# The level masks of a blockwise triangular inverse, applied by VectorE on the way out of PSUM

## The reference

```python
kk = jnp.einsum("bhncd,bhnsd->bhncs", k, k)
lower = jnp.where(strict, beta[..., :, None] * kk * decay, 0.0)
a_mat = jnp.broadcast_to(eye, lower.shape) + lower
sol = lax.linalg.triangular_solve(a_mat, rhs, left_side=True, lower=True, unit_diagonal=True)
```

## Time and profile before

| | |
|---|---|
| median of 3 runs | 3048.26 us (3047.57 to 3049.72) |
| profiled execution | 3046.6 us, span 3044.8 us |
| mean granted TensorE clock | 0.981 |
| TensorE busy | 2850.4 us, 94% of the span |
| GpSimd busy | 1728.8 us, 57% |
| VectorE busy | 1324.1 us, 43% |
| ScalarE busy | 1172.8 us, 39% |

### The profile page before, as it was taken

How to read it: one execution, slowest core, us unless ns; L and a number is a source line. 1 busy time by engine, 2 the same in 40 slices (tenths; PEclk the granted TensorE clock), 3 DMA queues, 4 the chain that set the end, 5 groups by cost and what they waited for, 6 DMA issues and landing times.

```text
span 3044.8 us, 37926 instructions
## 1 busy us (share of the span) xinstructions
PE 2850.4 (94%) x14376; PEld 2380.5 (78%) x14376; DVE 1324.1 (43%) x1864; ACT 1172.8 (39%) x2040; POOL 1728.8 (57%) x1324
## 2 busy tenths in 40 slices
PE   1799979999999999999999999999999999889998
PEld 1588767888888788888888788887888888668886
DVE  4555655353535335553434525545343432421123
ACT  2133443353444434353343433444333333343332
POOL 2254555575656656576555665657565655566554
PEclk9889999999999999999999999999999999999999
DMA  5521322222232323422233222422222222423332
GB/s 221 228 80 56 101 67 68 82 80 81 81 116 90 101 70 103 140 73 93 74 104 104 90 87 87 143 78 86 79 87 80 80 82 92 142 76 97 97 97 84
DMA packets 86581, 295.10 MB, mean 97 GB/s; under 512 B 10240, under 2 KB 10240, under 8 KB 82304
## 3 DMA queue, kind: packets, MB, share of 16 engines
q1 hardware_dynamic: 64944, 247.05, 25.6%
q10 hardware_dynamic: 21456, 45.62, 4.5%
HBM read 276.90 MB, written 15.73 MB: 96 GB/s over the span
## 4 chain that ended last, share of the span: by engine, by line
PE 83%; DVE 6%; POOL 5%; issue 2%; DMA 2%; ACT 2%; SPq 0%; ACTq 0%; POOLq 0%; DVEq 0%
PE acc L392 23%; PE acc L394 22%; PE acc L393 22%; PE pm L426 7%; PE pm L431 3%; DMA mixing<-in_ada_w 2%; POOL w L1388 1%; DVE mixing L1018 1%; POOL mT L1397 1%; ACT io L636 1%; PE pm L408 1%; PE pm L545 1%; DVE x L1257 1%; PE pm L518 1%; DVE io L934 1%
## 5 line engine op out<-in xcount | busy, mean ns | idle before, releaser
L1388 POOL TENSOR_TENSOR w<-raw,w 128x512 fp32r<-128x512 f32 x832 | 1116.4, 1344 | 1047.3 <-ACT w L610 1019.1
L610 ACT ACTIVATE w<-raw 128x512 fp32r<-128x512 f32 x832 | 521.0, 627 | 783.2 <-PE acc L394 662.3
L392 PE MATMUL acc<-mT,w 128*128 128x512 f32 x1280 | 517.3, 404 | 13.0 <-POOL mT L1397 5.8
L394 PE MATMUL acc<-mT,w 128*128 128x512 f32 x1280 | 501.6, 392 | 0.0
L393 PE MATMUL acc<-mT,w 128*128 128x512 f32 x1280 | 500.4, 391 | 0.0
L392 PE MATMUL acc<-hT,w 128*128 128x512 f32 x1024 | 437.1, 427 | 41.4 <-POOL w L1388 30.8
L394 PE MATMUL acc<-hT,w 128*128 128x512 f32 x1024 | 407.8, 398 | 0.0
L393 PE MATMUL acc<-hT,w 128*128 128x512 f32 x1024 | 406.7, 397 | 0.0
L1229 DVE SCALAR_TENSOR_TENSOR x<-acc,ab,x 128x512 f32<-128x512 f32 x256 | 191.4, 750 | 450.3 <-PE acc L394 450.1
L392 PE MATMUL acc<-hid,w 128*128 128x512 f32 x896 | 364.4, 407 | 13.8 <-POOL hid L1402 8.3
L394 PE MATMUL acc<-hid,w 128*128 128x512 f32 x896 | 350.3, 391 | 0.0
(11 more groups left out here) (201 smaller groups left out, 3828.0 us busy)
## 6 DMA issues: line engine op xcount, KB each, us to landing
raw<-in_w_all SPq DMA_DIRECT2D x416, 512.0 KB, 3.6
mixing<-in_ada_w SPq DMA_DIRECT2D x24, 1024.0 KB, 7.3
xr<-in_xT ACTq DMA_DIRECT2D x48, 256.0 KB, 2.9
out<-io ACTq DMA_DIRECT2D x32, 256.0 KB, 2.6
mixed_kept<-mixing ACTq DMA_DIRECT2D x28, 256.0 KB, 2.0
xr<-mixed_kept ACTq DMA_DIRECT2D x28, 256.0 KB, 2.7
x<-in_xT ACTq DMA_DIRECT2D x6, 1024.0 KB, 7.3
x<-in_xT SPq DMA_DIRECT2D x1, 2048.0 KB, 17.4
```

The costliest lines, as they stand in the source:

```text
L392: e.matmul(bank, whi, x[:, 0, :], start=first, stop=False)
L394: m = e.matmul(bank, wlo, x[:, 0, :], start=False, stop=last)
L610: e.activation(w2[:, 0, local % HALVES, :], raw[:, tile % NRAW, local % 2 * NT:(local % 2 + 1) * NT], ACT.Copy).then_inc(S["w_hi"], 1)
L1388: e.tensor_tensor(w2[:, 1, local % HALVES, :], raw[:, tile % NRAW, local % 2 * NT:(local % 2 + 1) * NT], w2[:, 0, local % HALVES, :].bitca ...
```

## The change

GpSimd no longer masks the operand. TensorE multiplies the whole `LT` by `T`, ScalarE's copy of that product goes away, and VectorE takes it out of PSUM with the mask of the level, `X = bE * lmask[l]`. The masks of levels 1 to 6 are those of the lower left blocks now, no longer transposed. The wait in front of the query convolution is on `x_out` in place of `lvl_mask`. The copy of `U` stays on ScalarE.

```diff
 TensorE, mix
                 if 22 <= s <= 42 and s % 4 == 2:
                     l = (s - 22) // 4 + 1
-                    e.wait_ge(S["lvl_mask"], (LEVELS - 1) * n + l)
                     if l == 1:
                         e.wait_ge(S["t_ready"], n + 1)
+                        e.wait_ge(S["lt_ready"], n + 1)
...
-                    four(bE, Lm, T).then_inc(S["x_out"], 1)
+                    four(bE, LT, T).then_inc(S["x_out"], 1)
 ScalarE, mix
-                if 22 <= s <= 42 and s % 4 == 2:
+                if 26 <= s <= 42 and s % 4 == 2:
                     l = (s - 22) // 4 + 1
-                    if l > 1:
-                        e.wait_ge(S["y_out"], (LEVELS - 1) * n + l - 1)
-                        e.wait_ge(S["t_turned"], (LEVELS - 2) * n + l - 1)
-                        e.activation(U, bF, ACT.Copy).then_inc(S["u_turned"], 1)
-                    e.wait_ge(S["x_out"], (LEVELS - 1) * n + l)
-                    e.activation(X, bE, ACT.Copy).then_inc(S["x_ready"], 1)
+                    e.wait_ge(S["y_out"], (LEVELS - 1) * n + l - 1)
+                    e.wait_ge(S["t_turned"], (LEVELS - 2) * n + l - 1)
+                    e.activation(U, bF, ACT.Copy).then_inc(S["u_turned"], 1)
 VectorE, front
                 if s == 42:
-                    e.wait_ge(S["lvl_mask"], (LEVELS - 1) * m)
+                    e.wait_ge(S["x_out"], (LEVELS - 1) * m)
                     conv(m, 1, GQ, (0, 1))
 VectorE, mix
+                if 22 <= s <= 42 and s % 4 == 2:
+                    l = (s - 22) // 4 + 1
+                    e.wait_ge(S["x_out"], (LEVELS - 1) * n + l)
+                    e.tensor_tensor(by_sub(X), by_sub(bE), over_subs(lmask[:, l, :]), ALU.mult).then_inc(S["x_ready"], 1)
 GpSimd, mix
-                if 18 <= s <= 38 and s % 4 == 2:
-                    l = (s - 18) // 4 + 1
-                    if l == 1:
-                        e.wait_ge(S["u_first"], n + 1)
-                    else:
-                        e.wait_ge(S["x_out"], (LEVELS - 1) * n + l - 1)
-                    e.tensor_tensor(by_sub(Lm), by_sub(LT), over_subs(lmask[:, l, :]), ALU.mult).then_inc(S["lvl_mask"], 1)
```

More of the change, by code:

```diff
@@ L175 @@
 gt_out sqk_ready sqq_ready ss_steps nk_ready k_nat kt_out kt_ready v_nat
-kk_out attn_ready lt_ready lvl_mask u_first t_first_out t_ready x_out x_ready y_out t_next u_next
+kk_out attn_ready lt_ready u_first t_first_out t_ready x_out x_ready y_out t_next u_next
 negc_ready gfac gvar rvar silu_v mod_steps gates_done kd_ready ks_out r_ready tr_out vnew_ready upd_out g_state o2_out
@@ L504, in mix @@
                         e.wait_ge(S["attn_ready"], n + 1)
-                        e.wait_ge(S["lt_ready"], n + 1)
                     if l < LEVELS - 1:
@@ L1526, in constants @@
         m = 1 << l
-        masks[:, 4 + l] = ((r[:, None] // (2 * m) == r[None, :] // (2 * m))
-                           & (r[:, None] // m % 2 == 0) & (r[None, :] // m % 2 == 1))
+        below = ((r[:, None] // (2 * m) == r[None, :] // (2 * m))
+                 & (r[:, None] // m % 2 == 1) & (r[None, :] // m % 2 == 0))
+        masks[:, 4 + l] = below if l else below.T
     inv = (10000.0 ** (-np.arange(0, DK, 2, dtype=f) / f(DK))).astype(f)
```

## The result

The changed kernel takes 3054.47 us in the median of 20 runs (3048.49 to 3057.45), the kernel before 3047.62 us in 20 runs on the same chip. The ratio is 1.002, with a 95% interval of 1.0013 to 1.0027: 6.85 us slower, just over the 0.2% that a measurement of this kernel tells from nothing. The prediction was 3055.5 us and +7.2 us. The profiled execution took 3053.98 us, with a span of 3052.2 us.

What follows compares the result with a forecast made beforehand. TensorE, busy 94% of the span, was taken as the bound, so only its waits and clock could move the time. The terms summed to +7.2 us, giving 3055.5 us, own range 3053 to 3060, wider range 3043.5 to 3064.

Steps and rivals of the forecast that it cites:

- units 6 and 10: Slot 43: VectorE's diagonal L923 pushed back by turns with GpSimd, TensorE waiting 3.0 us longer in each, +6.0 us.
- Relief in units 4, 8 and 12: Slot 44: without GpSimd's mask L1451, TensorE's wait for the low halves (L1388) goes, -1.86 us each, -5.6 us.
- The 1.5 us that I let L1148 give back: Three slots after the relief, TensorE waits for L1148's column: 0.5 us in each of three units, +1.5 us.
- Unit 2, slot 43: X pushes L1018 behind GpSimd's L1426 and the diagonal L923 behind one more GpSimd operation: +1.7 us.
- Units 0, 1 and 3: Block 0: later L1118 in slot 46 of units 0 and 1, +0.35 us each; later L1115 in unit 3, slot 42, +1.2.
- the sum: All terms added: 6.0 + 1.7 + 0.7 + 1.2 - 5.6 + 1.5 - 1.7 + 3.4 = +7.2 us.
- rival B: Relief wins: GpSimd's operations come earlier, VectorE meets none in slots 42 and 43; -7.7 us, 3040.6 us; chance 0.12.
- The clock: TensorE's low-clock stretches: one gone after unit 12's wait, -1.7 us; two new behind units 2, 6 and 10, +3.4 us.
- the signs to look for: TensorE's wait for L923 rises from 15.5 to about 23 us, L1388's falls 4 to 6; unit 6's L923 starts after 969.
- A: Rival: gains and losses cancel, with no new low-clock stretch and L1148 in time; +2.3 us, 3050.6 us; chance 0.24.
- C: Rival: VectorE bounds slots 42 to 47, L1148 late by 1 us or more in nine units; 3063 us; chance 0.13.
- D: Rival: the change does nothing, X is never waited for and the convolution has room; 3048.3 us; chance 0.08.

Runs made afterwards that it cites:

- L1426 later: Changed kernel with GpSimd's product for the query moved from slot 42 to slot 44: 3044.80 us, ratio 0.9992 to the kernel before.
- the runs on level 6: Kernel before with level 6 alone changed: 3054.54 us; changed kernel with level 6 alone put back as before: 3050.78 us.
- the masks kept: Changed kernel with GpSimd's six masks a unit still made into Lm, which no product reads: 3064.56 us, ratio 1.0058 to the kernel before.
- the hold alone: Kernel before with only the query convolution's wait in slot 42 changed, to TensorE's level 6 product instead of GpSimd's mask: 3048.35 us.

## Why the prediction held, and where it did not

**The clearest term, units 6 and 10.** Predicted: L923 ends 5.40 us after the product of level 6 (970.15 and 964.75), +3.0 us of waiting in each. Measured: product at 966.23, L919 ends at 971.55, 5.32 us after it; the waits rose by 2.90 us each. The order of turns is the one that was written down, pair by pair. The run with L1426 later shows that the turns make a good part of the size: with the same queue on VectorE, 1.96 us of the 2.90 us went.

The Trainium skill, "SBUF — State Buffer", section "Who interferes with whom", says of VectorE with two inputs in SBUF that it contends with a GpSimd operation that reads SBUF, and with at most one input there, outside the modes that use both ports, that it does not. The traces agree on both: L919 takes 1.75 us beside one and 0.68 us without, and L1106 takes 678 to 694 ns in all 96. L1011, a multiply of one tensor by scalars, waits as well (1.33 us in place of 0.49); whether it runs in such a mode, no run shows.

**Relief in units 4, 8 and 12.** Predicted -1.86 each; measured -1.60, -1.58 and -1.60. The 1.5 us that I let L1148 give back did not come: its waits are 0.9 us in 3, before and after. Instead TensorE's wait for L1402, later in the same units, grew from 1.3 us to 1.5 us each. Sum -4.8 and +0.5, for -4.1 predicted net. The cause is shown by the runs on level 6, and it is the mask of slot 38 that rows 8 showed.

**Unit 2, slot 43.** Predicted +1.7, measured +0.19. This is the step that failed most clearly. I took the operations in front of X as fixed and pushed all behind it by 0.68 us. But the last two taps of the value convolution, in front of X, take 2.50 us in place of 3.27 and end at 388.98 instead of 390.06; X came into the gap. The time line of unit 2 after the change:

```profile
387.33 1.65 DVE L1014 SCALAR_TENSOR_TENSOR mixing<-pg,para,mixing 128x512 f32<-128x512 f32 x1
...
389.25 0.69 DVE L1106 TENSOR_TENSOR mixing<-pm,lmask 128x512 f32<-128x512 f32 x1 [0.27 <-PE pm L426]
...
391.04 1.75 DVE L919 TENSOR_TENSOR io<-consts,small 128x512 f32<-128x512 f32 x1
```

L919 starts at 391.04, and started at 391.16 before. With level 6 alone changed, GpSimd still makes its five other masks, and there TensorE waits 4.23 us, 1.48 us more than before and near the +1.7. So the term holds or fails by what GpSimd does in front. Which of its operations makes the difference was not tested.

**Units 0, 1 and 3.** Units 0 and 1 cost 0.02 us each at slot 46, for 0.35 each predicted. Unit 3 was to lose 1.2 us in slot 42; it lost 0.04 there, but its idle time rose by 2.2 us, in three places that I had not named: 0.67 us for VectorE's L957, 0.75 us for X itself, and 0.76 us more for L1118. All of block 0 came to +1.8 us, for the +3.6 us of the sum.

**A term that was put at nothing.** The kernel before also waits for VectorE's L1136, behind the chain of slot 28, in units 0, 1 and 2:

```profile
PE pm L431 <- DVE mixing L1136: 1.5, 3, 1.2
```

After the change this wait is gone, and it is gone in the kernel with level 6 as before too, but not with level 6 alone changed. So it is the change of levels 1 to 5 that gives 1.5 us back in block 0. The sum has nothing for it; only rival B had the term, at 1.5 us.

**The clock.** Predicted: two new stretches at the lower level behind the waits of units 2, 6 and 10 (+3.4), and one less in unit 12 (-1.7). The stretches behind units 6 and 10 came, and unit 12's went. Two others came too, in units 7 and 11, behind waits of 1.87 and 1.91 us that had been there before with 1.84 and 1.79 us. Behind unit 2's wait, counted among the two, none came. Windows of the changed kernel, behind the waits of units 6, 7 and 10:

```profile
971.90:975.30 3.40, 3.40 (x7) 2.01 (x6) 1.06 (x2) 0.00 (x0) 0.00 (x0) 0.50 0.00 0
...
1255.20:1258.60 3.40, 3.40 (x9) 2.54 (x8) 2.91 (x5) 0.32 (x1) 0.00 (x0) 0.50 0.36 140
...
1688.70:1692.10 3.40, 3.33 (x6) 2.01 (x7) 1.43 (x3) 0.00 (x0) 0.00 (x0) 0.50 0.00 0
```

0.50 is the lower level, 1.2 GHz. Units 7 and 11 are 1.7 us longer each by this alone, with no more idle time. The start and the end, which the change hardly touches, together came to -0.9 us.

**The sum.** By stages, with the clock in each: block 0 came out 1.8 us under its terms, units 6 and 10 0.4 us under (+9.0 for +9.4), the relief 0.1 us under (-5.9 for -5.8), the start and the end at -0.9 us for nothing, and units 7 and 11 at +3.4 us for nothing. That leaves +0.2 us, and +7.4 for +7.2, partly by terms that cancel. By kind the sum does not hold: it had +5.5 us of waiting and +1.7 us of clock, and the profiles have +1.4 us and +6.0 us. That the total came within half a us is luck; the cause of the loss in units 6 and 10 is not.

Of the signs to look for, two came as written: L923's waits 21.6 us (about 23), and L919 in unit 6 from 969.80 (after 969). L1388's waits went down by 7.0 us, more than the 4 to 6; 1.6 us of that lies before unit 0. Of the rivals, A needed the clock to stay, and it fell. B needed L923 of unit 6 under 0.8 us, and it took 1.75, though its term for L1136 came. C is refuted by the waits for L1148, which did not change, and D by units 6 and 10.

## What to carry to other kernels

Price a moved operation where it lands, by what stands behind it in its engine's order: here 0.69 us of work and an earlier wait cost 2.9 us, since together they put three other operations into turns with GpSimd, and moving the one that TensorE waits for ahead of the rest turned 6.85 us of loss into a gain of 5.8 to 8.5 us. Split a change by level or place before judging it: five of the six levels gave nothing in the steady blocks, and the sixth held both the gain and the loss. And where two engines take turns, look at how often the pair meets, not only at the busy time: with 127 us of unused masks put back on GpSimd, VectorE's same instructions took 27 us longer.

## What the runs showed of the hardware that I had not expected

The clock does not answer to a wait of given length in one way. Behind the same wait of 3.31 us it fell to 0.50 in both units of the changed kernel, and in one of the two units each in the kernels with level 6 alone and with the masks kept, here unit 6 and unit 10 of the latter:

```profile
982.30:985.70 3.40, 3.40 (x18) 2.62 (x17) 0.97 (x2) 0.00 (x0) 0.00 (x0) 1.00 0.02 5
1696.80:1700.20 3.40, 3.34 (x6) 2.02 (x7) 1.42 (x3) 0.00 (x0) 0.00 (x0) 0.50 0.00 0
```

Behind waits of 1.79 to 1.92 us it fell in some executions and not in others, at places that the edits don't touch. Nor does unit 2's wait leave the clock alone, as the earlier trace rows had it and rival A took it: in eight of the twelve profiled executions the clock falls there, among them the one with the hold alone, where the wait is 2.75 us as before:

```profile
393.20:396.60 3.40, 3.40 (x9) 2.10 (x9) 2.10 (x2) 0.00 (x0) 0.80 (x1) 0.50 0.02 5
```

What decides it was not settled. Each time costs 1.7 us, so a difference of one or two such stretches can't be put down to an edit without a look at the granted clock. It fits with this that the changed kernel's runs lie in two groups, six of 20 from 3048.5 to 3050.3 us and the others from 3052.6 to 3057.5: the mean granted clock is 0.981 in all of the six, and 0.978 to 0.980 in the others. Only one of these runs has a trace, so in which units the two groups part was not seen.
